# Shift and scale of two layers as row sums on VectorE, feature tiles first, tables later

## What is computed

```python
c_act = silu(c)                                  # (1, 1024)
for l in range(2):                               # layer A
    mod = c_act @ w_ada[l] + b_ada[l]            # (1, 3072)
    shift, scale, gate = split(mod, 3)
    h = rms_norm(x, norm_g[l]) * (1 + scale) + shift
    proj = h @ w_in[l]                           # pool, q, k, v, rwkv, gates
    # pooling, retention (rotary by positions), rwkv
    merged = sum(sigmoid(gates) * (branches @ w_branch[l]))
    x = x + gate * (merged @ w_out[l])
x = rms_norm(x, final_g)
for l in range(2):                               # second block
    x = layer_norm(ALPHA * x + 0.5 * swiglu(x, w_gu, w_down))
    x = layer_norm(ALPHA * x + mixer(x))
    x = layer_norm(ALPHA * x + 0.5 * swiglu(x, w_gu, w_down))
```

## Time and profile before

| | us |
|---|---|
| median of 3 runs | 3770.73 (3768.35 to 3771.65) |
| profiled execution | 3767.53 |
| its span, first to last instruction | 3765.7 |
| PE busy | 3485.5 (93%), 17128 instructions |
| PEld busy | 2821.3 (75%) |
| DVE busy | 1703.4 (45%), 2431 instructions |
| ACT busy | 1125.3 (30%), 1645 instructions |
| POOL busy | 193.9 (5%) |
| mean granted TensorE clock | 0.960 |

### The profile page before, as it was taken

The page is one execution under the profiler, slowest core; times in us unless marked ns, Lnnn a source line. Parts: engine busy times, 40 slices in busy tenths (PEclk is TensorE's granted clock), DMA queues, the critical chain, the costliest instruction groups (busy, mean ns, idle before and its releaser), DMA issues.

```text
span 3765.7 us, 43155 instructions
## 1 busy us (share of the span) xinstructions
PE 3485.5 (93%) x17128; PEld 2821.3 (75%) x17128; DVE 1703.4 (45%) x2431; ACT 1125.3 (30%) x1645; POOL 193.9 (5%) x222
## 2 busy tenths in 40 slices
PE   8999888989899898999999988999999999889999
PEld 7777777767677677778888755888888887568887
DVE  2644454436544553345332565533253326754333
ACT  2432223323342222223332233332123213333321
POOL 1000000001000000000000110000000002100000
PEclk8999999999999999999999988999999999799999
DMA  4222112223222111122323211233222322013232
GB/s 175 84 74 67 51 62 68 73 79 115 65 76 73 53 55 40 51 84 90 101 95 107 86 38 45 86 100 107 95 89 96 106 95 73 28 56 101 96 109 75
DMA packets 83514, 303.18 MB, mean 81 GB/s; under 512 B 9696, under 2 KB 9968, under 8 KB 83312
## 3 DMA queue, kind: packets, MB, share of 16 engines
q1 hardware_dynamic: 77920, 282.59, 22.6%
q0 software_dynamic: 5392, 17.83, 1.4%
HBM read 295.66 MB, written 4.72 MB: 80 GB/s over the span
## 4 chain that ended last, share of the span: by engine, by line
PE 46%; DVE 5%; ACT 1%; issue 1%; POOL 0%; DVEq 0%; POOLq 0%; ACTq 0%
PE bank L522 15%; PE bank L524 14%; PE bank L523 14%; DVE acc L1141 2%; PE bank L528 1%; DVE xn L1141 1%; PE bank L1095 1%; PE bank L1119 1%; ACT pr L1948 1%; DVE wlo L1135 1%; DVE hl L1135 0%; DVE pr L1909 0%; ACT L1948 0%; POOL stat L2460 0%; DVE stat L1746 0%
## 5 line engine op out<-in xcount | busy, mean ns | idle before, releaser
L522 PE MATMUL bank<-hh,whi 128*128 128x512 f32 (+1 forms) x2704 | 1090.4, 403 | 55.1 <-DVE mrg L1135 12.6
L524 PE MATMUL bank<-hh,wlo 128*128 128x512 f32 (+1 forms) x2704 | 1042.0, 385 | 0.0
L523 PE MATMUL bank<-hl,whi 128*128 128x512 f32 (+1 forms) x2704 | 1041.5, 385 | 0.0
L1135 DVE TENSOR_TENSOR wlo<-raw,whi 128x1024 fp32r<-128x1024 f32 x498 | 610.4, 1226 | 913.2 <-ACT whi L1953 852.2
L1953 ACT CAST whi<-raw 128x1024 fp32r<-128x1024 f32 x514 | 539.9, 1050 | 792.5 <-PE bank L524 734.1
L522 PEld LDWEIGHTS bank<-hh,whi 128*128 128x128 f32 x2704 | 523.8, 194 | 193.5 <-issue 68.3
L524 PEld LDWEIGHTS bank<-hh,wlo 128*128 128x128 f32 x2704 | 522.9, 193 | 101.4
L523 PEld LDWEIGHTS bank<-hl,whi 128*128 128x128 f32 x2704 | 525.0, 194 | 81.4 <-issue 1.9
L522 PE MATMUL bank<-whi,fh 128*128 128x512 f32 x704 | 279.6, 397 | 0.0
L524 PE MATMUL bank<-whi,fl 128*128 128x512 f32 x704 | 279.1, 396 | 0.0
L523 PE MATMUL bank<-wlo,fh 128*128 128x512 f32 x704 | 279.0, 396 | 0.0
(11 more groups left out here) (324 smaller groups left out, 3909.6 us busy)
## 6 DMA issues: line engine op xcount, KB each, us to landing
raw<-in_W SPq DMA_DIRECT2D x514, 512.0 KB, 3.3
bc<-in_ln_g POOLq DMA_DIRECT2D x6, 512.0 KB, 4.4
bc<-in_ln_b POOLq DMA_DIRECT2D x6, 512.0 KB, 5.6
xn<-in_x SPq DMA_DIRECT2D x4, 512.0 KB, 7.4
AR<-in_W SPq DMA_DIRECT2D x2, 1024.0 KB, 11.4
mrg<-in_W SPq DMA_DIRECT2D x2, 1024.0 KB, 13.4
xn<-in_x POOLq DMA_DIRECT2D x4, 512.0 KB, 5.2
xd<-xn POOLq DMA_DIRECT2D x4, 512.0 KB, 3.6
```

The source lines that it names most:

```text
L522: e.matmul(out, ah, bh, start=first, stop=False, skip_group_check=True)
L523: e.matmul(out, ah, bl, start=False, stop=False, skip_group_check=True)
L524: return e.matmul(out, al, bh, start=False, stop=last, skip_group_check=True)
L1135: return self.e.tensor_tensor(o, a, b, op)
```

## The change

1. `first` of layer 0: the shift and scale columns are formed by VectorE. W holds c as a broadcast row (unit 0, into `gate`) and w_ada transposed, 128 output features to a unit (two units for each feature tile d). `gate` becomes silu(c). `weigh` is a tensor_tensor_reduce: product of a unit with `gate`, its row sum into one column of mod. Feature tile after feature tile gets its shift and scale, its hh, and its hl, and TensorE does all four units' products for tile d before d + 1. `TensorE.early`, `part` and `mod_part` go. In the order of instructions a `weigh` reads as two rows ISA, the product and the read of its sum.
2. Columns of layer 1: 16 transposed units are fetched to raw slots between the others (`columns_of`), and VectorE weighs them there (`column`, called from `ahead`). ScalarE and TensorE do nothing for them. SIDE changes from 345 to 337 for layer 0, and the 24 side steps of `ada(1, range(4))` become 16 empty ones. `ada(0, (4, 5))` waits for the last of them, since it writes into `gate`.
3. Angle tables: VectorE's 18 operations lie between those of rwkv of layer 0, in mrg, sgr and cosr; ScalarE's `sines` stand at its end, and two products of branch 0 wait for them. POOL stores `rot` during retention of layer 0 and loads it for layer 1 only.
4. SP issues cols, the c row, three raw units, ident, x, two early tiles, a raw unit, the six others, misc and positions. Three units are halved before x is scaled.
5. `alloc` rounds each width up to 32 floats, and there is a gap of 224 floats ahead of fh.

The diff, cut to its core:

```diff
+LINE = 32
...
+        if isinstance(pieces, int):
+            out[n] = w[:, 128 * pieces:128 * pieces + 128].T
+            continue
...
     def alloc(self, ctx, name, width, dt=F32):
-        return ctx.enter_context(self.nc.sbuf_tensor(name, [128, width], dt))
+        room = -(-width // LINE) * LINE
+        return ctx.enter_context(self.nc.sbuf_tensor(name, [128, room], dt))[:, 0:width]
...
+        self.early = [x for y in (self.mrg, self.AR, self.BH, self.VN, self.KH, self.pt1) for x in
+                      (y[:, j:j + 2048] for j in range(0, y.shape[1], 2048))]
...
+        d("gap", 224)
...
-SIDE = (345, 321)
+SIDE = (337, 321)
...
+        while self.next_raw < len(kinds):
+            if not kinds[self.next_raw]:
+                self.column(self.next_raw)
+                self.next_raw += 1
+            elif self.n_halved <= self.n_taken + RING - 1 and (self.n_halved < RING or self.n_halved - RING in self.spent):
+                self.one()
+            else:
+                break
...
-        return itertools.chain(self.ada(l + 1, range(4)) if l + 1 < DEPTH else iter(()), self.ada(l, (4, 5)))
+        return itertools.chain(self.columns_of(l + 1) if l + 1 < DEPTH else iter(()), self.ada(l, (4, 5)))
...
-    def early(self, bank, pairs):
-
-        k = self.k
-        for n in pairs:
-            q = EARLY_Q[n // 2]
-            self.wait_ge(("wd", n), ("cact",))
-            for j in range(4):
-                d = 4 * (n % 2) + j
-                for m in range(4):
-                    w = k.early[n][:, j * 512 + m * 128:j * 512 + (m + 1) * 128]
-                    t = self.e.matmul(bank[:, 4 * q + m:4 * q + m + 1], w, k.cact[:, d:d + 1], start=n % 4 == 0 and j == 0 and m == 0,
-                                      stop=d == 7, skip_group_check=True)
-            if n % 4 == 3:
-                t.then_inc(*self.up(("adc", n // 4)))
...
+    def columns_of(self, l):
+        k = self.k
+        for o in range(16):
+            k.units.append(("w_ada", (l,), o))
+            k.ring_of.append(None)
+            k.column_of.append(o)
+            k.kinds.append(False)
+            yield
...
-        mod = self.bank(self.adas, ("adc",))
-        self.early(mod, (0, 1))
...
+        jobs = [(key,) + self.coming(name, index, p) + (self.bank(self.all4, key),) for key, p in zip(keys, pieces)]
+        for d in range(8):
+            c = slice(128 * d, 128 * d + 128)
+            for key, wh, wl, i, bank in jobs:
+                self.wait_ge(("hi", i), ("lo", i), ("hd", d), ("ld", d))
+                t = self.three(bank[:, :], wh[:, c], wl[:, c], HALF(k.hh, d), HALF(k.hl, d), d == 0, d == 7)
+                if d == 7:
+                    t.then_inc(*self.up(key, ("used", i)))
+            if d < 4:
+                self.turn_x(4 + d)
...
+        self.spare = self.angles()
+        self.wait_ge(("sigr",), ("crow0",))
+        self.tt(k.gate[:, :], k.gate[:, :], k.xs[:, 3072:4096], ALU.mult).then_inc(*self.up(("crow",)))
+        for _ in range(3):
+            self.one()
...
+    def weigh(self, w, l, o, key):
+
+        self.e.tensor_tensor_reduce(w, w, self.k.gate[:, :], 1.0, 0.0, ALU.mult, ALU.add, self.k.mod[l][:, o:o + 1]).then_inc(
+            *self.up(key))
+
+    def column(self, n):
+        self.wait_raw(n)
+        self.wait_ge(("crow",))
+        self.weigh(self.k.raw_unit(n), 1, self.k.column_of[n], ("tr", n))
...
+        for d in range(8):
+            for j in range(2):
+                self.wait_ge(("wd", d))
+                self.weigh(k.early[d][:, 1024 * j:1024 * j + 1024], 0, 8 * j + d, ("td", d, j))
+            self.wait_ge()
+            self.tt(two(mod[:, 0:16], d), two(mod[:, 0:16], d), two(k.cols[:, ba:ba + 16], d), ALU.add).then_inc(*self.up())
+            self.wait_ge()
+            self.stt(mod[:, 16 + d:17 + d], mod[:, 8 + d:9 + d], 1.0, k.cols[:, ng + d:ng + d + 1], ALU.add, ALU.mult).then_inc(
+                *self.up(("modd", d)))
+            if d:
+                low(d - 1)
+        low(7)
...
+                self.wait_ge(y, ("bs", l, n, m), *([("sin", 1)] if l == n == 0 and m > 5 else []))
...
+            drain(self.spare)
+            self.wait_ge(("sin", 1))
+            self.ts(k.sinr[:, :], k.sinr[:, :], k.misc[:, 1:2], -1.0, ALU.mult, ALU.mult).then_inc(*self.up(("tab",)))
...
+            if p and not l:
+                next(self.spare, None)
...
+        self.wait_ge(("crow0",))
+        self.act(k.xs[:, 3072:4096], k.gate[:, :], ACT.Sigmoid).then_inc(*self.up(("sigr",)))
+        for _ in range(3):
+            self.one()
...
+        for d in range(8):
+            self.wait_ge(("xT", d), ("modd", d))
...
+            self.wait_ge(key, *([] if q == 5 else [("xo", l - 1, 1, 3)] if l else [("tr", max(n for n in range(len(k.kinds)) if not k.kinds[n]))]))
...
+    def sines(self, l):
+
+        k = self.k
+        for i, (o, x) in enumerate(((k.cosr[:, :], k.cosr[:, :]), (k.sinr[:, :], HALF(k.mrg, 6)))):
+            self.wait_ge(("ang", i))
+            self.act(o, x, ACT.Sin).then_inc(*self.up(("sin", i)))
...
+            self.wait_ge(*((("tr", n - RAW),) if i is None else (("hi", i), ("lo", i))))
...
+        self.load(k.gate[:, :], A["W"][0], ("crow0",))
+        for n in range(RAW):
+            self.fetch(n)
         self.load(k.ident[:, :], A["ident"], ("ident",))
         for t in range(4):
             self.load(k.x_tile(t), A["x"][0][t * 128:(t + 1) * 128, :], ("x0", t))
         self.early(0)
         self.early(1)
-        self.fetch(0)
-        self.fetch(1)
-        self.early(2)
-        self.early(3)
-        self.fetch(2)
-        self.fetch(3)
-        for n in range(4, 8):
-            self.early(n)
-        for n in range(4, len(k.kinds)):
+        self.fetch(RAW)
+        for d in range(2, 8):
+            self.early(d)
+        self.load(k.misc[:, :], A["misc"], ("misc",))
+        self.wait_ge(("td", 1, 1))
+        self.load(HALF(k.mrg, 6).bitcast(I32), A["positions"][0].partition_broadcast(128), ("pos",))
+        for n in range(RAW + 1, len(k.kinds)):
```

More of the change, by code:

```diff
@@ L432, in one @@
         self.next_raw += 1
+    def column(self, n):
+        pass
+    def columns_of(self, l):
+        for _ in range(16):
+            yield
     def take(self):
@@ L597, in program @@
     def program(self):
-        for q in EARLY_Q:
-            for ui in range(4):
-                self.k.units.append(("w_ada", (0,), n_pieces(256 * ui, 512 * q)))
+        self.k.units.append(("c", (0,), None))
+        for d in range(8):
+            self.k.units += [("w_ada", (0,), d), ("w_ada", (0,), 8 + d)]
         for l in range(DEPTH):
@@ L685, in ada @@
             bank = self.bank(self.adas, ("adT", l, q))
-            self.wait_ge(("adr", l, q), ("ones",))
-            if q < 4:
-                for i in range(4):
-                    t = self.e.matmul(bank[:, i:i + 1], k.gate[0:2, 512 + i * 128:640 + i * 128], k.ones[0:2, 0:1], start=True,
-                                      stop=True, skip_group_check=True)
-            else:
-                self.wait_ge(("gateb", l, q))
-                t = self.e.matmul(bank[:, :], k.ones[0:3, :], k.gate[0:3, 512:1024], start=True, stop=True)
+            self.wait_ge(("adr", l, q), ("ones",), ("gateb", l, q))
+            t = self.e.matmul(bank[:, :], k.ones[0:3, :], k.gate[0:3, 512:1024], start=True, stop=True)
             t.then_inc(*self.up(("adT", l, q)))
@@ L1225, in mod_part @@
         mod = k.mod[0]
[L1226 to L1242 removed]
+        two = lambda x, d: x.rearrange("p (a b) -> p a b", a=2)[:, :, d:d + 1]
+        low = lambda d: self.lower(HALF(k.hl, d), k.RT[d][:, :], HALF(k.hh, d), [("hd", d), ("vd", d)], [("ld", d)])
+        for d in range(8):
+            for j in range(2):
+                self.wait_ge(("wd", d))
+                self.weigh(k.early[d][:, 1024 * j:1024 * j + 1024], 0, 8 * j + d, ("td", d, j))
+            self.wait_ge()
+            self.tt(two(mod[:, 0:16], d), two(mod[:, 0:16], d), two(k.cols[:, ba:ba + 16], d), ALU.add).then_inc(*self.up())
+            self.wait_ge()
+            self.stt(mod[:, 16 + d:17 + d], mod[:, 8 + d:9 + d], 1.0, k.cols[:, ng + d:ng + d + 1], ALU.add, ALU.mult).then_inc(
[3 more added lines that the diff above has]
+        low(7)
         return [self.take() for _ in range(4)]
@@ L1257, in mod_columns @@
         mod = k.mod[l]
-        self.wait_ge(("modc", l, 3), ("cols",))
+        self.wait_ge(("cols",))
         self.tt(mod[:, 0:16], mod[:, 0:16], k.cols[:, ba:ba + 16], ALU.add).then_inc(*self.up())
@@ L2007, in ada @@
             self.wait_ge(key)
-            if q < 4:
-                self.e.copy(k.mod[l][:, 4 * q:4 * q + 4], k.bank(key)[:, 0:4]).then_inc(*self.up(("modc", l, q), ("free", key)))
-            else:
-                self.e.copy(HALF(k.gate, q - 4), k.bank(key)[:, :]).then_inc(*self.up(("gate", l, q - 4), ("free", key)))
+            self.e.copy(HALF(k.gate, q - 4), k.bank(key)[:, :]).then_inc(*self.up(("gate", l, q - 4), ("free", key)))
```

(9 more changed lines are left out.)

184 lines of the change are left out of this document (71 added, 113 removed).

## The result

| | before | changed |
|---|---|---|
| median, four runs each | 3771.18 us | 3735.05 us (3731.82 to 3745.61) |
| ratio of the two | | 0.9911 (0.989 to 0.9931) |
| profiled execution, its span | 3767.53, 3765.7 | 3745.61, 3743.8 |
| mean granted clock | 0.960 | 0.952 |

The change is worth 36 us. 79 were forecast, and 3735 lies above the end of the range, 3722. That it would be faster was right. The profiled execution is the slowest of its four.

What follows compares the result with a forecast made beforehand. It took TensorE's small work to bound the start and TensorE to be mostly busy in the chunk stages. Terms -37.5 - 1 + 1.5 + 2.6 - 21 - 24 = -79.4 gave 3691 us, range 3673 to 3722.

Steps and rivals of the forecast that it cites:

- Start: In `first` of layer 0, shift and scale leave TensorE for VectorE's row sums: -37.5 us.
- Layer 1's columns: In layer 0's chunk stage, TensorE and ScalarE lose the column work, VectorE trades subtractions for sums: -21 us.
- table loads: Without Sin at the start, ScalarE's two table switches at 100 us fall away: -1 us.
- rival b: TensorE's clock or later landings take half of the start's gain, leaving some -19: 3710 us, chance 0.09.
- Angle tables: 18 VectorE operations move into rwkv of layer 0, +1.5 us; table load and Sin at its end, +2.6.
- Sin part: At the end of layer 0's rwkv, VectorE's mrg waits for ScalarE's table load and two Sin: +2.6 us.
- Alignment: SBUF starts at multiples of 128 bytes make matmuls with fh, oh, mh and xh faster: -24 us.
- Rival (a): Rounding does nothing for speed; the tiles differ in something else, such as place in memory: 3715 us, chance 0.14.
- Rival (d): Layer 0's chunk stage is bound by its chains and gives 8 us instead of 21: 3704 us, chance 0.09.

Runs made afterwards that it cites:

- e5: The changed kernel run again unaltered, for a second profile: 3732.39 us, ratio 0.9919 to the kernel before.
- e1: Kernel before with only the rounding of SBUF tensors to 32 floats and the gap ahead of fh: 3752.15 us, ratio 0.9962.
- e12: e1 without the gap of 224 floats ahead of fh: 3763.67 us, one execution.
- e2: Changed kernel with layer 1's columns computed on TensorE and ScalarE as before: 3723.69 us, ratio 0.9893 to the kernel before.
- e3: Changed kernel with each of layer 1's 16 row sums cut to an operation on one column: 3721.17 us, ratio 0.9882 to the kernel before.
- e7: Changed kernel with one more VectorE operation of a sum's length ahead of each of layer 1's 16 row sums: 3756.76 us, ratio 0.9982.
- e13: e6 with layer 0's gate steps begun 16 places later in the side stream, no empty steps: 3730.98 us, ratio 0.9908 to the kernel before.
- e6: Changed kernel with layer 1's 16 row sums moved into rwkv of layer 0, no empty steps, gate's steps first: 3706.35 us, ratio 0.9849.
- e14: e1 with 32 floats ahead of raw, so the tensors start 256 bytes past a multiple of 2048: 3747.77 us, one execution.
- e11: e1 with rounding to 16 floats instead of 32: 3758.42 us, one execution.

## Why the prediction was wrong

**Start: right.** -37.5 forecast. Layer 1's columns apart, everything up to rwkv's first matmul with wa moved from 109.1 to 69.3 (e5), 39.8 us with the table loads' 1. The steps behind it held too: sums of 1.226 us and a tile in 3.65 (from one hl to the next; 3.9 was taken), the first product at 32 (33), full speed from the second tile on (so rival b falls), end at 59.4 (62.2). The next unit came at 62.41 (62.6), but behind a wait for pt that had been forecast for nobody. That this number fits is in part luck.

**Angle tables: right in kind, 2 us low.** rwkv took 209.7 instead of 203.6 from the same matmul on, 6.1 for 4.1. The Sin part was exact, 2.64.

**Alignment: right in direction, its size 14 instead of 24, its condition wrong.** fh gave its part, 16 (16.9 was worked out). The steps for oh, mh and xh, 11 us by duration of which 7 were kept, gave nothing that the profiles show (e1). And the condition as put, multiples of 128 bytes, was too weak: without the gap, which the forecast passed over, the ffn's second product keeps 1.2 of its 4.0 us (e12). Rival (a), that something other than this alignment sets the tiles apart, such as their place in memory, had that part right.

**Layer 1's columns: wrong, +11 instead of -21** (chunk stage 574.7 against 563.7; by medians the changed kernel is 9 us behind e2). This step made 32 of the 44 us by which the sum was off; alignment made 11. Its errors, as the prediction put them:
- "VectorE trades 16 wlo of 1.27 for 16 sums of 1.38, +2". The trade isn't even. A sum's time counts where it stands, 0.7 us each and 1.5 for the next (e3, e5, e7). All that went, the 16 subtractions among it, gave 9.8 together (e13).
- "18 us on an engine that is busy for 90% of this stage", taken as gain. The 18 were right as busy time: with the work for the columns gone altogether, TensorE was busy for 17.9 us less (e13 against e2). But it was idle for 8.1 more, so the stage gave 9.8 us, ScalarE's part included. In the changed kernel it was busy for 16.5 us less than before and idle for 27.5 more (e5).
- "the chunk stage of layer 1, which does the same without such columns", 33.8 us shorter, was taken as the other bound. It doesn't do the same in the same order: there the gate's steps come first, here they stand behind 24 steps before the change and behind 16 after it. This place alone was worth 18.5 us of layer 0's stage (e13 against e6), which the change couldn't give.

Rival (d), chain-bound, was the right one. Its gain of 8 is near the 9.8 that e13 shows for the removal. Left out was what the change puts into the same stage: the sums, the passage through the raw slots and the empty steps, together 18.5 us. The range missed since it let the chunk term end at a gain, though for an edit that also adds work to a stage with waits both signs stood open.

**Sum for e5's profile** against the one of before: -39.8 (start) + 6.1 (rwkv) + 11.0 (chunk stage) + 2.6 (its w_out stage, 86.5 instead of 83.9, at a clock of 0.96 instead of 1.00) - 15.7 (four ffn products), together -35.8; the spans differ by 34.8. Each term is a difference of two profiles. Up to the same matmul with wa the kernels with the old start took 101.9 to 109.2 us (e14, e11), so the start's -39.8 is good to a few us.

## What to carry to other kernels

Work taken from an engine pays only where that engine ends last. In a stage where a chain hops between engines, what stands in a queue just ahead of the chain's short operations decides, and a step that merely moves can cost as much as one that is added: compare the order at the waits, and give the term both signs. A second stage is a bound for the first only if it has the same order too. And one variant that is much better can be so for another reason than its name says. e6 gains 26 us over the change, but the sums cost 15 us or more in rwkv too. What e6 gains is mostly the early place of the gate's steps. Whether that place is open to a kernel with the sums in the chunk stage wasn't tried; there the gate's steps write into the buffer that the sums read.

## What the runs showed of the hardware

- A 128x512 matmul's duration depends on where its operands stand in SBUF. A median of 389 ns (390 for a few) was read in every layout where both stand at the same place within 2048 bytes (128 or 256 past a multiple). At other places 392 to 398 was read but for one, fl in e11, with 388. For a stage that TensorE fills, that was 124.9 us before against 120.9 in e1.
- A tensor_tensor_reduce of 128x1024 with two float32 sources in SBUF takes 1.226 us and its accumulator's read 0.08, the same as a plain subtraction of that size.
- A stage of the same instructions can run at another granted clock. The mh stage took 83.9 us at 1.00 before and 85.9 at 0.94 in e1, with nothing changed but start addresses, and the stage behind it gave 2.2 us back. What set the clock isn't shown.
- Executions of one kernel can differ in one stage alone: the changed kernel's chunk stage was 589.0 us at a clock of 0.91 in one profile and 574.7 at 0.94 in another, in the same order of instructions.
